# A two-block transformer kernel: value tile of the attention moved, gate scans regrouped, accumulator cleared in pieces, a projection moved into the last head

## What is computed

```python
def even_mixer(h, ...):
    p = h @ w_in
    da_q, da_k, da_v, da_z, ml_qk, ml_v, ml_i, ml_f, ml_o, ml_z = split(p)
    o_a = diff_attention(da_q, da_k, da_v, lam)       # 8 causal heads, two softmaxes each
    y_a = rmsnorm(o_a, da_head_g) * (1 - lam_init) * silu(da_z)
    qk = silu(causal_dwconv(ml_qk, conv_w, conv_b))   # 4 taps over time
    hm = mlstm_chunkwise(*split(qk), ml_v, ml_i + b_igate, ml_f + b_fgate)   # 4 heads
    y_b = rmsnorm(hm * sigmoid(ml_o), ml_head_g) * silu(ml_z)
    return concat(y_a, y_b) @ w_out
```

## Time and profile before

| | us |
|---|---|
| median of three runs | 2995.83 |
| lowest and highest | 2994.35 and 3000.58 |
| the profiled execution, whole | 2994.34 |
| its span on the core | 2992.5 |
| head 1 to head 6, from one head to the next | 86.0 |

### The profile page before, as it was taken

One profiled execution on the slowest core, in us unless ns is written; L12 is line 12 of the kernel. 1 busy time (PEld: TensorE's weight loads), 2 busy tenths in 40 slices (PEclk: granted clock), 3 DMA queues, 4 the chain that ended last, 5 costly groups with the idle time before them and its releaser, 6 DMA issues.

```text
span 2992.5 us, 38708 instructions
## 1 busy us (share of the span) xinstructions
PE 2827.6 (94%) x14522; PEld 2262.6 (76%) x14522; DVE 1390.7 (46%) x2147; ACT 773.0 (26%) x1390; POOL 1205.3 (40%) x571
## 2 busy tenths in 40 slices
PE   7899999999988899999987999999989999999997
PEld 3588888888866677777765888888768888888885
DVE  6433433343364556555555654635440144444445
ACT  3600000000044333333332222232433321112112
POOL 0444444444443422222211334434254365555554
PEclk9999999999999899999998999999999999999999
DMA  9211111111112000101100111111232211111113
GB/s 384 75 50 49 49 49 45 46 49 49 42 50 71 22 30 28 35 28 35 35 21 15 57 50 49 49 49 50 78 113 93 94 60 66 61 56 56 56 64 120
DMA packets 58223, 185.27 MB, mean 62 GB/s; under 512 B 17300, under 2 KB 17428, under 8 KB 55976
## 3 DMA queue, kind: packets, MB, share of 16 engines
q1 hardware_dynamic: 37152, 152.68, 14.9%
q10 hardware_dynamic: 21000, 31.61, 3.0%
HBM read 163.22 MB, written 21.05 MB: 62 GB/s over the span
## 4 chain that ended last, share of the span: by engine, by line
PE 81%; DVE 9%; issue 4%; ACT 4%; DMA 1%; POOL 1%; DVEq 0%; ACTq 0%; SPq 0%; POOLq 0%
PE ps L663 25%; PE ps L665 24%; PE ps L664 24%; PE ps L1003 2%; DVE acc L2071 1%; PE ps L804 1%; PE ps L731 1%; PE ps L1014 1%; DVE stat L2222 1%; DMA resid<-x_t 1%; PE ps L837 1%; DVE da_p L2233 1%; DVE da_al L2242 1%; ACT ps L1679 1%; ACT sg_g L1875 1%
## 5 line engine op out<-in xcount | busy, mean ns | idle before, releaser
L510 POOL TENSOR_TENSOR slab_hi<-slab_raw,zero 128x1024 fp32r<-128x1024 f32 x227 | 434.7, 1915 | 1526.8 <-PE ps L665 1439.2
L663 PE MATMUL ps<-h_hi,slab_hi 128*128 128x512 f32 x2512 | 997.1, 397 | 30.6 <-DVE h_lo L2032 11.8
L665 PE MATMUL ps<-h_hi,slab_lo 128*128 128x512 f32 x2512 | 983.3, 391 | 0.0
L664 PE MATMUL ps<-h_lo,slab_hi 128*128 128x512 f32 x2512 | 983.2, 391 | 0.0
L663 PEld LDWEIGHTS ps<-h_hi,slab_hi 128*128 128x128 f32 x2512 | 474.7, 189 | 142.2 <-issue 19.3
L512 POOL TENSOR_TENSOR slab_lo<-slab_raw,slab_hi 128x1024 fp32r<-128x1024 f32 x227 | 573.6, 2527 | 17.9
L665 PEld LDWEIGHTS ps<-h_hi,slab_lo 128*128 128x128 f32 x2512 | 474.1, 189 | 101.1
L664 PEld LDWEIGHTS ps<-h_lo,slab_hi 128*128 128x128 f32 x2512 | 475.1, 189 | 93.8
L2071 DVE TENSOR_TENSOR acc<-ps,acc 128x512 f32<-128x512 f32 x352 | 228.7, 687 | 23.9 <-PE ps L665 22.6
L2078 DVE TENSOR_TENSOR ffn_p<-ps,ffn_g 128x1024 f32<-128x1024 f32 x22 | 27.0, 1226 | 454.2 <-PE ps L665 448.3
L2069 DVE SCALAR_TENSOR_TENSOR resid<-ps,mod,resid 128x512 f32<-128x512 f32 x320 | 212.8, 744 | 0.0
(11 more groups left out here) (320 smaller groups left out, 3777.7 us busy)
## 6 DMA issues: line engine op xcount, KB each, us to landing
slab_raw<-w_in SPq DMA_DIRECT2D x168, 512.0 KB, 3.6
mod_big<-mod_w SPq DMA_DIRECT2D x12, 2048.0 KB, 12.0
slab_raw<-w_c SPq DMA_DIRECT2D x43, 512.0 KB, 3.5
res_scr<-resid ACTq DMA_DIRECT2D x4, 2048.0 KB, 7.2
resid<-res_scr ACTq DMA_DIRECT2D x2, 4096.0 KB, 13.1
gv_scr<-sg_t ACTq DMA_DIRECT2D x16, 512.0 KB, 2.6
slab_raw<-gv_scr SPq DMA_DIRECT2D x16, 512.0 KB, 3.5
resid<-x_t SPq DMA_DIRECT2D x2, 2048.0 KB, 15.3
```

Source lines behind the costliest of these rows:

```text
L510: pool.tensor_tensor(hi, raw[slot][:], zeros, ALU.add).then_inc(hi_done.sem, 1)
L663: pe.matmul(dst, w_h, r_h, start=first, stop=False, skip_group_check=True)
L664: pe.matmul(dst, w_h, r_l, start=False, stop=False, skip_group_check=True)
L665: return pe.matmul(dst, w_l, r_h, start=False, stop=last, skip_group_check=True)
```

## The change

- `v_t` is placed behind `p_0` instead of ahead of `v_hi`, so that it lies beyond the residual's 32 KB; `v_hi` to `p_0` move down by 4 KB. ACT's wait for `spill` moves from ahead of `da_v_half(0, e)` to ahead of `da_q_half(0, e)`.
- The four parts of the gates leave head 0: parts 0 and 1 follow the two query low halves, parts 2 and 3 stand between the two key low halves. POOL's three exponents move from behind the split of slab IN_DA+7 to behind that of IN_DA+3. ACT's `gate_rows` moves from step 7 to step 2 of head 0.
- `acc` is cleared by eight memsets of 1024 columns, one after another.
- The last head does Z where the other heads do, and projects slab IN_ML (it stands where a next V slab would) in the two V places. ACT copies it to `v_t`, and the convolution of the queries reads it there. Its first two steps come ahead of `da_norm`.
- Behind the last head PE does slab IN_ML+1 in quarters: one, the squares, one, the spread, two.

```diff
         q_hi, q_lo, k_hi, k_lo = (take(f"da_{n}", [P, T], F32R)[0] for n in ("qh", "ql", "kh", "kl"))
-        v_t = take("da_vt", [P, T])[0]
         v_hi, v_lo = (take(f"da_{n}", [P, KT, P], F32R)[0] for n in ("vh", "vl"))
         da_z = take("da_z", [P, T])[0]
         p_0 = [take(f"da_p0{b}", [P, T])[0] for b in range(2)]
+        v_t = take("da_vt", [P, T])[0]
...
+            def gate_exponents():
+                pool.wait_ge(g_dve.sem, GATE_STEPS)
...
             for s in range(1, 8):
                 split_in(IN_DA + s, s % 2, (IN_DA + s) // 2)
                 if s == 1:
                     split_low(1, range(2 * KT))
-            pool.wait_ge(g_dve.sem, GATE_STEPS)
...
+                if s == 3:
+                    gate_exponents()
+
             pool.wait_ge(g_st.sem, 16 * 5)
-            pool.memset(acc[:], 0.0).then_inc(acc_zero.sem, 1)
+            for k in range(KT):
+                pool.memset(acc[:, k, :], 0.0).then_inc(acc_zero.sem, 1)
...
-                if not last:
-                    da_half(h, DA_Z_SLAB, 0, range(0, KT // 2))
+                da_half(h, DA_Z_SLAB, 0, range(0, KT // 2))
...
-                da_half(h, DA_Z_SLAB, 0 if last else 1)
+                da_half(h, DA_Z_SLAB, 1)
...
-                if last:
-                    da_half(h, DA_Z_SLAB, 1, range(0, KT // 2))
-                else:
-                    pe.wait_ge(a_z.sem, a_z.at(h, 0))
-                    da_half(h + 1, DA_V_SLAB, 0)
+                pe.wait_ge(a_z.sem, a_z.at(h, 0))
+                da_half(h + 1, DA_V_SLAB, 0)
...
             da_values(DA_HEADS - 1, KT // 2 - 1)
-            project(IN_ML, 0)
+            project_quarter(IN_ML + 1, 1, 0)
             da_squares(DA_HEADS - 1, last=True)
-            project(IN_ML + 1, 1, between=lambda: da_spread(DA_HEADS - 1, last=True))
+            project_quarter(IN_ML + 1, 1, 1)
+            da_spread(DA_HEADS - 1, last=True)
+            for part in (2, 3):
+                project_quarter(IN_ML + 1, 1, part)
...
-                    if i in (1, 2) and not last:
+                    if i in (1, 2):
                         da_v_half(h + 1, i - 1)
...
-                    if i == KT - 1 and first:
+                    if i == 2 and first:
                         gate_rows()
...
-            act.wait_ge(spill.sem, spill.at(0))
             for e in range(2):
                 da_v_half(0, e)
...
+            act.wait_ge(spill.sem, spill.at(0))
             for e in range(2):
                 da_q_half(0, e, True)
...
-                    if first and i < 4:
-                        gates(i)
...
             for e in range(2):
                 da_q_low(0, e)
-            for e in range(2):
-                da_k_low(0, e)
+                gates(e)
+            da_k_low(0, 0)
+            for part in (2, 3):
+                gates(part)
+            da_k_low(0, 1)
...
-            dve.wait_ge(in_mm.sem, in_mm.at(IN_ML))
+            dve.wait_ge(a_v.sem, a_v.at(DA_HEADS))
+            for j in range(2):
+                conv_step(0, 0, j, v_t[:])
             da_norm(DA_HEADS - 1)
-            for j in range(CONV):
-                conv_step(0, 0, j)
+            for j in range(2, CONV):
+                conv_step(0, 0, j, v_t[:])
```

More of the change, by code:

```diff
@@ L558, in _ @@
             low_part(f_hi, f_lo, F_TILES - 1, ffn_lo[1], ffn_p, ffn_hi[1])
+            def gate_exponents():
+                pool.wait_ge(g_dve.sem, GATE_STEPS)
+                by_chunk = lambda col: col.to_broadcast([ML_HEADS, NC, CHUNK])
+                pool.tensor_tensor(g_d[:], g_max[:], by_chunk(g_m[:, 0:NC].unsqueeze(2)), ALU.subtract).then_inc(g_exp.sem, 1)
+                pool.tensor_tensor(g_d2[:], g_cum[:], g_max[:], ALU.add).then_inc(g_exp.sem, 1)
+                pool.tensor_tensor(g_d3[:], g_u[:], by_chunk(g_max[:, :, CHUNK - 1:CHUNK]), ALU.subtract).then_inc(g_exp.sem, 1)
             split_c(C_GATES)
@@ L1071, in da_head @@
                     mm.then_inc(a_vtr.sem, 1)
-                if not last:
-                    da_half(h, DA_Z_SLAB, 0, range(KT // 2, KT))
+                da_half(h, DA_Z_SLAB, 0, range(KT // 2, KT))
                 if out:
@@ L1094, in da_head @@
                 da_scores(h, 3)
[L1095 to L1099, removed]
+                pe.wait_ge(a_z.sem, a_z.at(h, 1))
+                da_half(h + 1, DA_V_SLAB, 1)
                 da_turn(h, 3, 0)
                 da_scores(h, 4)
-                if not last:
-                    pe.wait_ge(a_v.sem, a_v.at(h + 1))
+                pe.wait_ge(a_v.sem, a_v.at(h + 1))
                 if out:
@@ L1647, in da_head @@
                         da_z_half(h, 0, first)
-                        if not last:
-                            da_z_half(h, 1, first)
+                        da_z_half(h, 1, first)
                     if i < 2:
@@ L1658, in da_head @@
                             da_high(h - 1, e)
-                    if i in (1, 2) and not last:
+                    if i in (1, 2):
                         da_v_half(h + 1, i - 1)
-                    if i == 2 and last:
-                        da_z_half(h, 1, first)
                     if not last and i in (4, 6):
@@ L2279, in da_head @@
                     if out and i == 3:
-                        dve.wait_ge(acc_zero.sem, 1)
+                        dve.wait_ge(acc_zero.sem, KT)
                     if i >= 4:
@@ L2341, in _, with conv_step @@
             da_gate(DA_HEADS - 1, 1)
-            def conv_step(h, which, j):
-                dst, x = (mt, kt)[which], PS[which]
+            def conv_step(h, which, j, source=None):
+                dst, x = (mt, kt)[which], PS[which] if source is None else source
                 col = lambda tap: par[:, bass.ds(h + (COL["conv_w"] + 8 * tap + 4 * which), 1)]
@@ L2535, in _ @@
             dve.wait_ge(const.sem, 15)
-            dve.wait_ge(acc_zero.sem, 2)
+            dve.wait_ge(acc_zero.sem, KT + 1)
             def sg_weights(g):
```

## The result

| | median, us | lowest to highest | runs |
|---|---|---|---|
| before | 2997.42 | 2994.35 to 3000.58 | 4 |
| after | 2979.59 | 2977.67 to 2984.32 | 4 |

The ratio is 0.9939, with a 95% interval of 0.9926 to 0.9953: the changed kernel is faster by 18 us. Its profiled execution took 2980.28 us, with a span of 2978.6.

The account below looks back on a forecast made before the run. TensorE's (PE's) gaps and slow stretches were taken as what can give time back. 5.1 - 3.1 + 1.0 + 7.1 + 0.8 + 11.0 - 0.9 = 21.0 off 2994.34 gave 2973.3, stated as 2974.0; range 2965 to 2983.

Parts of the forecast that it names:

- Value tile: Opening: PE's 3.49 us gap before the query projection and the slow matmuls behind it go, 5.1 us gained.
- Gates ahead of the first maxima: Opening: DVE's gate steps, slowed by a POOL split, delay head 0's first maxima; 3.1 us given back.
- `gate_rows`: Head 0, step 3: ACT's rows, 4.86 us, take what DVE gives back, so 0 gained; 4.8 if hidden.
- Part 3: Head 0: the gates' part 3 no longer holds the maxima of step 5, 1.0 us gained.
- Memset: Accumulator cleared earlier, in eight pieces: head 1 opens as head 3 does, 25.74 - 18.64 = 7.1 us gained.
- Last head: Filled last head runs like head 3, 0.8 us gained; the full projection pass behind it leaves, 11.0 more.
- The stop at the spread: Behind the last head: PE waits at the spread, 0.9 us lost, ends 0 and 3.
- Rival 1: Opening pays in full as ACT's rows and POOL's splits hide: + 3.1 + 4.8, so 2966; 10%.
- Rival 2: Opening pays nothing: DVE meets the whole split, slab IN_DA+4's split comes late, `gate_rows` holds step 3 longer: 2979; 18%.
- Rival 3: The last head's filling stretches it, up to 10.9 us of the projection come back: 2985; 6%.
- Rival 4: PE stays at the lower clock through the tail and first recurrent head, up to 3003; 2%.
- Rival 5: Opening: PE waits for the query read-out, not the value tile, so the 5.1 stays: 2979, counted in rival 2.

Follow-up runs that it names:

- gates in head 0: Changed kernel with gate scans, POOL's exponents and ACT's `gate_rows` back in their old places in head 0, eight memsets at head 1's start: 2982.24 us, ratio 0.9937.
- rows split: Changed kernel with ACT's gate-row exponentials in step 1 and DMA issues in step 2 of head 0, each ahead of the value half there: 2968.86 us, ratio 0.9899.
- the run alone: Kernel before with only the filled last head and the quarters behind it, nothing at the opening: 2986.25 us, ratio 0.9955.
- part 3 late: Changed kernel with gate rows split over steps 2 and 3, the gates' part 3 in step 0 of head 0, POOL's exponents one split later: 2971.28 us, ratio 0.9902.
- value tile only: Kernel before with only the value tile moved and ACT's wait for the residual's copy put behind the gate inputs: 2994.97 us, ratio 0.9983.
- second set: The changed kernel run again, unchanged, beside three other runs: 2979.28 us, ratio 0.9930.
- the two batches: The two groups of follow-up runs; the kernel before had medians of 3000.46 us in the first and 3000.64 us in the second.

## Why the prediction was right

The likeliest time was 2974.0, in a range of 2965 to 2983; the median was 2979.59. By the terms, starts measured from the copy:

- **Value tile, 5.1.** Measured 5.3 alone and 5.3 in the change. The cover that was counted at 0.7 (query read-out before PE needs it) held: ACT had the query half at 916.47, in a profile that was 1.4 late at the copy, so at the 915.1 that was counted.
- **Gates ahead of the first maxima, -3.1.** DVE took 16.1 us for the gates and two low halves (917.86 to 933.93), and 12.2 + 1.4 + 2.5 = 16.1 was counted. Inside, two errors cancel. The eight scans lost 3.0 to the split (6.54 - 3.52), not 2.5; and the 12.2 held 1.71 for a step that takes 1.21 here, since in the earlier trace rows it was already stretched beside a split (POOL's half of 947.49 + 1.89 ran into it). Of the split's 4.8 us (918.79 to 923.6) the scans met 3.6, so it was close to exclusion where the two met; beside the step at 918.18 it was the split that gave way (2.37 instead of 1.89). The Trainium skill (SBUF — State Buffer, "Who interferes with whom") says that a DVE instruction with two SBUF inputs contends with a GpSimd instruction that reads SBUF, and that one with at most one SBUF input, outside DVE's two-port modes, does not; the scans and the low half at 919.43, which kept its 0.69, agree. The full 4.3 did not come, because less of the split lay beside such steps.
- What was mis-sized is how this reaches PE. The sum's own end is 932.6 and 933.2 with the last low half, yet the prediction took 934.5 for the maxima. They came at 934.57 in a profile 1.4 late, so at 933.2. The first scaling took 0.29 longer, as counted. PE's gap is 2.29 where 0.32 stood before (940.85), so 2.0 and not 3.1. But behind it run eight matmuls at 1.2 GHz, 940.50 to 943.89, 3.39 us for 1.8 at the higher level: 1.6 more. Together 3.6, and from the copy to the transposes behind it the changed kernel is 3.6 later than the run with the gates in head 0. The prediction priced slow matmuls where it took a gap away and forgot them where it made one.
- **`gate_rows`, 0.** PE waits 5.17 there, against 4.85 before: DVE's wait turned into ACT's, to the half microsecond. The run with the rows split shows the cause, and the prediction's own figure of 4.8, "if ACT's work hid", came to 5.1 at the values of step 3 and 5.8 at head 1's first score.
- **Part 3, 1.0.** The gap before step 5 is 1.59 instead of 2.62.
- **Memset, 7.1.** Measured 7.1, with the scaling in head 1 at 0.28 as foretold. The prediction counted place and pieces together. The runs part them: the place is enough for all of it, the pieces in the old place give 4.0 (alone) or 5.6 (with the gates in head 0). Pieces were costed at 0 to 0.9 in step 7, and a scaling of 1.48 stands there instead of 0.75; one memset costs 0.4 of that too. This term was left at 0 and should have been 0.4 to 0.7 (PE's gap there is 3.18 instead of 2.45, and 2.87 with one memset). It did not show in the sum, because before had a slow stretch of eight matmuls behind that gap (from 1009.1), worth 1.6, and this profile has none: that is luck.
- **Last head, 0.8 and 11.0 - 0.9.** Between head 1's spread and the key turn 11.1 in the first profile, 10.6 in the second and in the run alone; 10.9 was foreseen. The last head by itself gave 0.5, not 0.8 (45.13 us where 44.91 was counted and before had 45.66). The stop at the spread is 0.31 and not 0.9. The match holds for profiles in which the last values run at the higher level, as in before; where they did not, 7.4 (gates in head 0) and 8.1 (part 3 late) are left against before, and 11.0 if the former is set against value tile only, in which they did not either.

So the sum inside the changed stretch, 21.0, was measured as 21.6 and 21.2. The mechanisms are the foreseen ones, but that the total fits to 0.6 owes something to chance: the 0.5, 0.3 and 0.7 that were missed in head 0 were made up by the slow stretch of 1.6 that before had and the changed kernel's profiles have not. The first profile then took 1328.8 us from the key turn to the end, where before took 1322.5; by that and the 1.4 at the copy it ends 7.0 above the forecast of its own time, 2973.3. That the median came out 5.6 above 2974.0 for the same reason is likely and not shown, since the other three executions have no trace; their mean clocks are 0.982 to 0.984, and the execution of the second set that took 2973.99 has 0.987. The base had that spread too: its median was 2995.83 with three runs, 2997.42 with four, and 3000.5 and 3000.6 in the two batches. Against the last of these the second set of runs of the changed kernel is 21.4 faster.

Rival 1 (the opening pays in full) failed on ACT's rows as its own "against" said. Rival 2 gave 2979 and the median is there, but its mechanism did not happen: the split of slab IN_DA+4 ended at 944.4 in time, and the opening and head 0 together kept 3.4. Rival 3 left no trace: the last head is within 0.3 of head 3. Rival 4, the clock, shows in part: in two of the seven profiles with the new last head the last values run at the lower level, for 2.3 us more. But the same happens in two of three with the old one, and the projections behind are back at the higher level after at most two matmuls. Rival 5 (PE waits for the query read-out) is ruled out by value tile only, where the gap went.

## What to carry to other kernels

A step that is moved off one engine's way must be read on all engines: what DVE gave back in step 3 was taken by ACT's rows in the same place, and splitting these into two covered places was worth as much again as the whole opening. A gap taken away can give back the slow matmuls behind it, and a gap made can bring them; price both. And where one kernel's own profiles differ by 6 us in code that nobody touched, the effect of an edit is read from starts of the same instruction close on either side of the edit, not from the span, and more than one profile of the unchanged kernel is needed to say how good such a difference is.

## What the runs showed of the hardware

- DVE gets between back-to-back memsets of POOL. Behind one memset of 6.93 us a scaling of 128 columns took 5.43, behind eight pieces in the same place 0.34. The next scalings, 256 columns beside a piece and 384 beside the splits that follow, took 0.99 and 1.37; with nothing beside them they took 0.34 and 0.41 (changed kernel with one memset, 1027.82 and 1037.10). With the rows split, a scaling of 256 columns in head 0 (942.52) took 2.46 and ended as the low half of a split did (942.43 + 2.40); it cost PE nothing there.
- A gap of 2.3 us ahead of the second scores cost the same in four profiles: from its end to the twelfth matmul of the projection behind it, PE took 5.0 us in the changed kernel, its second profile and the one with one memset, and 4.8 with the rows split, against 3.4 behind a gap of 0.32 (gates in head 0). In three the lower level began at the fourth matmul of the projection, in the fourth at the scores. Elsewhere the same gap costs now this, now nothing: one of 2.45 in step 7 of head 0 was followed by eight slow matmuls before, and by none in value tile only and with the gates back in head 0; one of 3.2 by none in the changed kernel and by ten with part 3 late. The length of a gap alone does not tell what it costs.
- The 24 matmuls of the last values took 2.9 or 5.2 us behind the same gap of 1.41 (above).
- Whole stretches differ likewise: 0.88 and 0.95 of the clock over the same 100 us of code, 0.94 and 1.00 over another 60.
